# Sums of squares from the transposed input, and a first projection block scaled in two parts

## The reference, cut to what matters

```python
def rms_norm(x, w):
    xf = x.astype(jnp.float32)
    y = xf * lax.rsqrt(jnp.mean(xf * xf, axis=-1, keepdims=True) + EPS)
    return (y * w.astype(jnp.float32)).astype(x.dtype)
...
    h = rms_norm(x, norm_mix_w)
    proj = h @ w_in
```

## Time and profile before

| | |
|---|---|
| median of three runs | 2597.7 us (2597.64 to 2598.22) |
| the profiled execution | 2597.84 us, its span 2596.0 us |
| busy, share of the span | TensorE 98%, VectorE 84%, ScalarE 59%, GpSimd 13% |
| end of the first projection in the chain of waits | 41.82 us |

### The profile page before, as it was taken

One profiled execution on the slowest core, in us unless ns is written; L12 is line 12 of the kernel. 1 busy time (PEld: TensorE's weight loads), 2 busy tenths in 40 slices (PEclk: granted clock), 3 DMA queues, 4 the chain that ended last, 5 costly groups with the idle time before them and its releaser, 6 DMA issues.

```text
span 2596.0 us, 34033 instructions
## 1 busy us (share of the span) xinstructions
PE 2547.8 (98%) x13255; PEld 1981.7 (76%) x13255; DVE 2184.8 (84%) x2451; ACT 1537.9 (59%) x1773; POOL 334.6 (13%) x409
## 2 busy tenths in 40 slices
PE   7999999999999999899999999999999999999998
PEld 7898899889988888676767767766767677666665
DVE  5789888988887344899999999999999999999997
ACT  3444444454435121577777777777777777777775
POOL 0322332233321000000000000000000000000000
PEclk9999999999999999899999999999999999999999
DMA  4233233322447343999999999999999999999995
GB/s 157 70 117 122 89 101 104 130 92 95 135 135 260 131 150 114 373 394 375 379 372 381 377 370 379 376 377 374 374 381 372 376 376 378 375 377 371 373 377 208
DMA packets 72046, 705.22 MB, mean 272 GB/s; under 512 B 9616, under 2 KB 13840, under 8 KB 49360
## 3 DMA queue, kind: packets, MB, share of 16 engines
q1 hardware_dynamic: 48576, 628.95, 62.4%
q0 software_dynamic: 13952, 55.55, 6.9%
q10 hardware_dynamic: 9360, 18.55, 1.9%
HBM read 669.36 MB, written 33.67 MB: 271 GB/s over the span
## 4 chain that ended last, share of the span: by engine, by line
PE 95%; DVE 2%; DMA 1%; ACT 1%; issue 1%; ACTq 0%; POOL 0%; DVEq 0%; POOLq 0%
PE p_gu L2296 38%; PE p_y L2323 19%; PE pp L1042 17%; PE pp L1249 5%; PE pp L1086 5%; PE pp L1268 2%; PE pdg L1137 2%; PE p_h L2308 1%; PE off_banks L1120 1%; PE pp L1351 1%; PE ptr L1104 1%; PE off_banks L1134 1%; PE off_banks L1132 1%; DVE room L1452 0%; PE ptr L1285 0%
## 5 line engine op out<-in xcount | busy, mean ns | idle before, releaser
L2196 DVE TENSOR_TENSOR wl<-raw,wh 128x2048 fp32r<-128x2048 f32 x528 | 1194.1, 2290 | 115.9 <-ACT wh L2115 105.7
L2115 ACT ACTIVATE wh<-raw 128x2048 fp32r<-128x2048 f32 x528 | 991.0, 1911 | 235.0 <-PE p_y L2323 224.2
L2296 PE MATMUL p_gu<-wh,xh 128*96 128x512 f32 x1408 | 565.8, 402 | 0.0
L2296 PE MATMUL p_gu<-wh,xl 128*96 128x512 f32 x1408 | 555.1, 394 | 0.0
L2296 PE MATMUL p_gu<-wl,xh 128*96 128x512 f32 x1408 | 553.0, 393 | 0.0
L1042 PE MATMUL pp<-h_hi,wx_hi 128*128 128x256 f32 (+1 forms) x864 | 307.0, 355 | 3.5 <-DVE zs L1468 3.0
L2296 PEld LDWEIGHTS p_gu<-wl,xh 128*96 128x96 f32 x1408 | 227.2, 161 | 100.0
L2296 PEld LDWEIGHTS p_gu<-wh,xh 128*96 128x96 f32 x1408 | 227.3, 161 | 88.4 <-DVE wl L2196 1.2
L1042 PE MATMUL pp<-h_hi,wx_lo 128*128 128x256 f32 (+1 forms) x864 | 293.8, 340 | 0.0
L1042 PE MATMUL pp<-h_lo,wx_hi 128*128 128x256 f32 (+1 forms) x864 | 292.7, 339 | 0.0
L2296 PEld LDWEIGHTS p_gu<-wh,xl 128*96 128x96 f32 x1408 | 227.2, 161 | 83.2
(11 more groups left out here) (290 smaller groups left out, 3724.5 us busy)
## 6 DMA issues: line engine op xcount, KB each, us to landing
raw<-in_w_e SPq DMA_DIRECT2D x176, 3072.0 KB, 11.1
w_raw<-in_w_x SPq DMA_DIRECT2D x48, 512.0 KB, 3.5
dec<-acs POOLq DMA_DIRECT2D x48, 512.0 KB, 4.8
w_raw<-in_w_g SPq DMA_DIRECT2D x24, 512.0 KB, 3.5
g_tab<-gx POOLq DMA_DIRECT2D x8, 1152.0 KB, 5.9
w_raw<-in_w_s SPq DMA_DIRECT2D x16, 512.0 KB, 3.6
gx<-fo ACTq DMA_DIRECT2D x16, 384.0 KB, 3.0
ys<-yt ACTq DMA_DIRECT2D x14, 384.0 KB, 2.7
```

What stands on the lines that cost most here:

```text
L2115: act.activation(wh[:, n % 2, at:at + hi - lo], raw[:, n % RAW, lo:hi], ACT.Copy).then_inc(s_wh, 1)
L2196: dve.tensor_tensor(wl[:, n % 2, to], raw[:, n % RAW, lo:hi], wh[:, n % 2, to].bitcast(F32), ALU.subtract).then_inc(s_wl, 1)
L2296: mm = pe.matmul(p_gu[n % 2][0:SLOTS, 0:w], xx[:, side, k * SLOTS:(k + 1) * SLOTS], ww[:, n % 2, k * w:(k + 1) * w], start=(k == 0 and i = ...
```

## The change

The rows of x are not loaded any more. The squares are made from the transposed blocks: ScalarE squares each hT[k] into `sqT` (the last block in two parts, 512 and 256 tokens), VectorE adds the eight squares up block by block, TensorE multiplies the result for each 128 tokens by one column of ones, which sums over the partitions, and VectorE scales that sum (`ssq_x`); GpSimd keeps only the power. The transfers go out as six blocks of xT, the first weight block, two more blocks, the second weight block. The first block k = 0 is scaled, split and multiplied in two parts (tokens 0 to 511 and 512 to 767), each with its own count on the semaphores. The warm-up matmuls are placed anew: 13 on ones when the fourth block has landed, 5 behind the sums, 8 behind the broadcast. The wait for the second weight block's low part moves into the first part of the projection, and the Exp of a_log behind the copies.

```diff
@@ sync
-            for c in range(NT):
-                sp.dma_start(x_rows[:, c], A["x"][c]).then_inc(m_x[c], 16)
             for k in range(KD):
-                if 1 <= k <= 2:
-                    sp.dma_start(raw[:, k - 1], A["w_x"][0, k - 1]).then_inc(s_raw[k - 1], 16)
                 sp.dma_start(hT[:, k], A["xT"][k]).then_inc(m_xT[k], 16)
+                if k == 5:
+                    sp.dma_start(raw[:, 0], A["w_x"][0, 0]).then_inc(s_raw[0], 16)
+            sp.dma_start(raw[:, 1], A["w_x"][0, 1]).then_inc(s_raw[1], 16)
@@ gpsimd
-            pool.wait_ge(s_ssq, NT)
+            pool.wait_ge(s_neg, 1)
+            pool.wait_ge(s_rstd, 1)
             pool.sem_inc(s_go, 1)
-            row = Steps(pool, s_rstd)
-            row(pool.tensor_scalar(ssq_x[:], ssq_x[:], 1.0 / D, EPS, ALU.mult, ALU.add))
-            pool.wait_ge(s_neg, 1)
-            row(pool.tensor_tensor(rstd_x[:], ssq_x[:], neg_half[:], ALU.pow))
+            pool.tensor_tensor(rstd_x[:], ssq_x[:], neg_half[:], ALU.pow).then_inc(s_rstd, 1)
@@ scalar
-            for c in range(NT):
-                act.wait_ge(m_x[c], 16)
-                act.activation(x_rows[:, c, :], x_rows[:, c, :], ACT.Square, accum_out=ssq_x[:, c:c + 1]).then_inc(s_ssq, 1)
+            for k, lo, hi in squares:
+                act.wait_ge(m_xT[k], 16)
+                act.activation(sqT[:, k, lo:hi], hT[:, k, lo:hi], ACT.Square).then_inc(s_sqT, 1)
+            high(weight(0, 0))
+            high(weight(0, 1))
+            for i, (k, lo, hi) in enumerate(shares):
+                act.wait_ge(s_hT, i + 1)
+                act.activation(h_hi[:, k, lo:hi], hT[:, k, lo:hi], ACT.Copy).then_inc(s_hh, 1)
             act.wait_ge(m_const, 96)
             act.activation(ea[:], alog[:], ACT.Exp).then_inc(s_act, 1)
@@ tensor
+            pe.wait_ge(s_ones, 1)
+            pe.wait_ge(m_xT[3], 16)
+            for _ in range(13):
+                pe.matmul(pp[0][:, 0:P], ones[:], ones[:], start=True, stop=True)
+            for i, (lo, hi) in enumerate(parts):
+                pe.wait_ge(s_ssum, KD - 1 + i)
+                for c in range(lo // P, hi // P):
+                    mm = pe.matmul(p_ss[:, c:c + 1], sqT[:, KD - 1, c * P:(c + 1) * P], ones[:, 0:1], start=True, stop=True)
+            mm.then_inc(s_ssq, 1)
             pe.wait_ge(m_const, 96)
+            keep_warm(5, pp[0][:, 0:P])
+            pe.wait_ge(s_rstd, 2)
+            for lo, hi in parts:
+                for c in range(lo // P, hi // P):
+                    mm = pe.matmul(p_bc[:, c * P:(c + 1) * P], rstd_x[:, c:c + 1].to_broadcast([P, P]), ident[:],
+                                   start=True, stop=True)
+                mm.then_inc(s_rows, 1)
             keep_warm(8, pp[0][:, 0:P])
...
-            keep_warm(24, pp[0][:, 0:P])
-            pe.wait_ge(s_wl, weight(0, 1) + 1)
-            for k in range(KD):
-                pe.wait_ge(s_hl, k + 1)
+            pe.wait_ge(s_wl, weight(0, 0) + 1)
+            for i, (k, lo, hi) in enumerate(shares):
+                pe.wait_ge(s_hl, i + 1)
                 for j in range(2):
+                    if i == 0 and j == 1:
+                        pe.wait_ge(s_wl, weight(0, 1) + 1)
@@ vector
             dve.wait_ge(m_const, 96)
+            for i, (k, lo, hi) in enumerate(squares[1:]):
+                dve.wait_ge(s_sqT, i + 2)
+                if i:
+                    dve.wait_ge(s_ssum, min(i, KD - 2))
+                dve.tensor_tensor(sqT[:, k, lo:hi], sqT[:, k - 1, lo:hi], sqT[:, k, lo:hi], ALU.add).then_inc(s_ssum, 1)
+            dve.wait_ge(s_ssq, 1)
+            dve.tensor_scalar(ssq_x[:], p_ss, 1.0 / D, EPS, ALU.mult, ALU.add).then_inc(s_rstd, 1)
             low(weight(0, 0))
             low(weight(0, 1))
```

More of the change, by code:

```diff
@@ L163, in mixer @@
                 e = Alloc(nc, first)
-                x_rows = e.sb("x_rows", [P, NT, D])
+                sqT = e.sb("sqT", [P, KD, T])
                 hT = e.sb("hT", [P, KD, T])
@@ L241, in mixer @@
         p_bc = off_banks[:, 0:T]
+        p_ss = pdg_bank[:, 0:NT]
         p_dt, p_f, p_b, p_tot = (t[:, 0:NT * NH].rearrange("p (c n) -> p c n", c=NT)
@@ L282, in mixer @@
         s_pb, s_pt, s_cp, s_ch, s_picks, s_ia, s_idx = a.sems("c_pb", "c_pt", "c_cp", "c_ch", "c_picks", "c_ia", "c_idx")
-        m_x = a.sems(*[f"m_x{c}" for c in range(NT)])
         m_small, m_const, m_acs = a.sems("m_small", "m_const", "m_acs")
         m_xT = a.sems(*[f"m_xT{k}" for k in range(KD)])
-        s_ssq, s_rstd, s_rows, s_hT = a.sems("s_ssq", "s_rstd", "s_rows", "s_hT")
+        s_sqT, s_ssum, s_ssq, s_rstd, s_rows, s_hT = a.sems(
+            "s_sqT", "s_ssum", "s_ssq", "s_rstd", "s_rows", "s_hT")
         s_dt, s_dve, s_act, s_cum, s_cumT, s_copy = a.sems("s_dt", "s_dve", "s_act", "s_cum", "s_cumT", "s_copy")
@@ L289, in mixer @@
         s_neg, s_absv, s_ones, s_dA, s_de = a.sems("s_neg", "s_absv", "s_ones", "s_dA", "s_de")
-        prepared = (*m_x, *m_xT, m_small, s_ssq, s_rstd, s_rows, s_hT, s_dt, s_dve, s_act, s_cum, s_cumT, s_copy,
+        prepared = (*m_xT, m_small, s_sqT, s_ssum, s_ssq, s_rstd, s_rows, s_hT, s_dt, s_dve, s_act, s_cum, s_cumT, s_copy,
                     s_hh, s_hl, s_neg, s_absv, s_ones, s_dA, s_de)
+        parts = ((0, SEQS[0]), (SEQS[0], T))
+        shares = (*((0, *part) for part in parts), *((k, 0, T) for k in range(1, KD)))
+        squares = (*((k, 0, T) for k in range(KD - 1)), *((KD - 1, *part) for part in parts))
         def by_group(t):
@@ L959, in _ @@
             act.dma_start(alog[:], A["a_log"].partition_broadcast(P)).then_inc(m_const, 16)
-            for c in range(NT):
-                act.wait_ge(m_x[c], 16)
-                act.activation(x_rows[:, c, :], x_rows[:, c, :], ACT.Square, accum_out=ssq_x[:, c:c + 1]).then_inc(s_ssq, 1)
+            for k, lo, hi in squares:
[6 more added lines that the diff above has]
+                act.activation(h_hi[:, k, lo:hi], hT[:, k, lo:hi], ACT.Copy).then_inc(s_hh, 1)
             act.wait_ge(m_const, 96)
             act.activation(ea[:], alog[:], ACT.Exp).then_inc(s_act, 1)
-            high(weight(0, 0))
-            high(weight(0, 1))
-            for k in range(KD):
-                act.wait_ge(s_hT, k + 1)
-                act.activation(h_hi[:, k, :], hT[:, k, :], ACT.Copy).then_inc(s_hh, 1)
             act.wait_ge(s_zero, 1)
@@ L1334, in residual @@
                           start=True, stop=True).then_inc(s_ia, 1)
-            pe.wait_ge(m_const, 96)
-            keep_warm(8, pp[0][:, 0:P])
[L1338 to L1343, removed]
-            keep_warm(24, pp[0][:, 0:P])
-            pe.wait_ge(s_wl, weight(0, 1) + 1)
@@ L1348, in _ @@
+            for i, (k, lo, hi) in enumerate(shares):
+                pe.wait_ge(s_hl, i + 1)
                 for j in range(2):
-                    for n0, n1 in ((0, SEQS[0]), (SEQS[0], T)):
-                        for i, (w, h) in enumerate(three(wx_hi, wx_lo, h_hi, h_lo)):
+                    if i == 0 and j == 1:
+                        pe.wait_ge(s_wl, weight(0, 1) + 1)
+                    for n0, n1 in [(n0, n1) for n0, n1 in parts if lo <= n0 and n1 <= hi]:
+                        for x, (w, h) in enumerate(three(wx_hi, wx_lo, h_hi, h_lo)):
@@ L1351, in _ @@
                             mm = pe.matmul(pp[j][:, n0:n1], w[:, j, k * P:(k + 1) * P], h[:, k, n0:n1],
-                                           start=(k == 0 and i == 0), stop=(k == KD - 1 and i == 2))
+                                           start=(k == 0 and x == 0), stop=(k == KD - 1 and x == 2))
                     if k == KD - 1:
@@ L1869, in _ @@
             dve.wait_ge(m_const, 96)
+            for i, (k, lo, hi) in enumerate(squares[1:]):
[5 more added lines that the diff above has]
+            dve.tensor_scalar(ssq_x[:], p_ss, 1.0 / D, EPS, ALU.mult, ALU.add).then_inc(s_rstd, 1)
             low(weight(0, 0))
             low(weight(0, 1))
[L1872 to L1880, removed]
+            dve.wait_ge(m_const, 96)
+            for i in range(len(shares) + 1):
+                if i < len(shares):
+                    k, lo, hi = shares[i]
+                    if k == 0:
+                        dve.wait_ge(s_rows, i + 1)
+                    dve.scalar_tensor_tensor(out=hT[:, k, lo:hi], in0=hT[:, k, lo:hi], scalar=nmix[:, k:k + 1],
+                                             in1=p_bc[:, lo:hi], op0=ALU.mult, op1=ALU.mult).then_inc(s_hT, 1)
+                if i:
+                    k, lo, hi = shares[i - 1]
+                    dve.wait_ge(s_hh, i)
+                    dve.tensor_tensor(h_lo[:, k, lo:hi], hT[:, k, lo:hi], h_hi[:, k, lo:hi].bitcast(F32), ALU.subtract)\
                        .then_inc(s_hl, 1)
```

## The result

The changed kernel takes 2603.4 us (median of 22 runs, 2599.9 to 2604.6) against 2597.8 us for the kernel before (22 runs, 2595.4 to 2600.6). The ratio is 1.0021, with a 95% interval of 1.0016 to 1.0027: 5.5 us slower, 4.2 to 7.0. The forecast was 2.5 us slower: the direction is right and the size is half of the measured one. The measured time lies inside the whole range (2596.3 to 2603.5) by 0.1 us only, and outside the 2599.3 to 2601.2 of the forecast's own case, and the range reached that far for the sake of tables as late as before (13.4 us), which landed at 12.4; that it holds is partly luck. "Within 0.2%" had a chance of 0.87, and the measured ratio stands on that line, a hair over it. Of the rivals, the gain did not come, and the one with the low clock was true up to the broadcast and not in the projection.

A forecast was written before the change was run, and what follows sets the result against it. The end of the first projection's 96 matmuls (41.82 us) was taken to move everything behind it one to one; T 26.3 + 18.0 gave 44.35, +2.5 us, so 2600.2 us, with a range of 2596.3 to 2603.5.

The forecast's parts named there:

- the forecast's own case: Whole kernel: 2.5 us slower, 2600.2 us, own range 2599.3 to 2601.2; chance 0.45.
- tables as late as before: Rival at the start: alog still lands at 13.4 us, the rest as forecast; +4.45, 2602.1 us; chance 0.10.
- the gain: Rival before the adds: tables land by 9 to 10 us and do not gate them; -1.1, 2596.6 us; chance 0.17.
- the one with the low clock: Rival on TensorE: clock stays low into the projection, which ends at 49.4; +7.5, 2605.2 us; chance 0.10.
- The table wait: Head of VectorE's program: adds queue behind all six tables, start 11.5 us; squares alone would allow an earlier end, 2 us lost.
- One table for one piece: Transfer queues: tables and large pieces alternate, so alog lands behind the sixth xT, at 11.45 us instead of 13.4.
- The slow spot: Transfers at 10 to 11 us before the change: 128 GB/s, which could vanish and give 1 us more.
- The sums at the low clock: TensorE's one-column matmuls after some 5 us idle: 0.22 us per record at half clock, result at 20.95 us.
- Power: GpSimd's pow after the scaling: 1.34 us as before, ending at 22.75; VectorE's low parts covered by the broadcast wait.
- When the clock comes back: TensorE: dense work since 18.2 us brings the clock up by 23.3, so the broadcast's first 8 records cost 0.9.
- The split: First block in two parts: brings 0.8 plus 0.45 us, but TensorE then waits 1.0 us once behind k=0.
- T: Time the first h_lo of the projection's first block is ready, forecast 26.3 us; projection end forecast as T + 18.0.

The follow-up runs named there:

- no table wait: The changed kernel with VectorE's adds no longer behind the wait for the six tables; 2600.4 us, ratio 1.0007 to the kernel before.
- low parts early: The changed kernel with both low parts of the weights made on VectorE before it waits for the sum over partitions; 2602.6 us, ratio 1.0019.
- no split: The changed kernel with the first block scaled, copied and subtracted as one piece of 768 columns; 2603.2 us, ratio 1.0020.
- long warm-up: The changed kernel with 36 instead of 13 warm-up matmuls on ones; 2601.0 us, ratio 1.0017.
- all on the change: The changed kernel with broadcast tables late, no table wait before the adds, 20 warm-up matmuls on ones, one low part before the sum wait; 2597.5 us, ratio 1.0000.

## Why the prediction was right or wrong

- **The bound.** Right: the end of the first projection decides, one to one in the medians (table above), and the 24 warm-up matmuls hid 1.9 us where I had 2.0.
- **The table wait.** Right in kind, shown by taking it away (2.9 us at the sums). Mis-sized: alog at 11.45 forecast, 12.42 measured. The sixth xT landed at 11.5, as worked out; alog came 0.9 behind it and not 0.4. One table for one piece was the right choice over a fixed 10 us: alog's 8.9 us from issue to landing were 10.0 before. The Trainium skill ("DMA: Bandwidth & Descriptors", Queues, rings and completion order) has each engine change queues packet by packet; the trace agrees with it. The distance is no constant: in the four other kernels with the same transfers alog came 0.4 to 1.4 us behind the sixth xT. The slow spot, which I only kept as a possible 1 us, was the tables' own.
- **The adds.** 7.0 forecast, 7.08 measured (1.06 from start to start, not 0.99; the parts a little less).
- **The sums at the low clock.** 2.45 forecast behind the last add, 2.73 measured; at the high clock 1.50. That the clock falls was right, and was chosen from the earlier trace rows.
- **Power.** Mis-sized: 1.34 forecast, 2.08 measured. I counted the low parts as covered by the wait for the broadcast, which they were, and gave nothing to their work beside GpSimd; ahead of the sum they leave the power at 1.33 us. The broadcast started at 24.87 instead of 23.2: alog, the sums and the power are 1.0 + 0.3 + 0.7 us later than forecast, of which the wait behind five warm-up matmuls that I had put last hid 0.4.
- **When the clock comes back.** The largest error. I took 5.1 us from the start of the one-column records, as in before from its first warm-up, and so 23.3; it was 26.9. Their later start does not explain it: 19.57 + 5.1 would be 24.7, just ahead of the broadcast, and it took 7.3 us. In the three other traces in which the clock was low, or fell, as these records began it took 6.3 (no table wait), 8.5 (low parts early) and 8.2 us (no split). The broadcast's first eight records took 2.09 instead of 0.9 us. The one-column matmuls with a gap ahead of them did not hold the clock in the long warm-up either; why it took until 26.9 here is not isolated.
- **The split.** Right: gap behind the first k, T + 18.0 forecast, 18.2 measured. The net gain is 0.55 us or less by experiment, where the lead it takes away costs the rest.
- **Sum.** From T = 26.3 to 29.2: broadcast start 1.7 late, broadcast 1.2 longer, 0.1 in the steps; 44.35 became 47.40. The rival "low clock" was right for the warm-up and the broadcast's first eight records and wrong for the projection (49.4), before which the clock was back; its ten per cent should have been more, and with it the chance of over 0.2%. The range held because it went up to 2603.5 for another reason, tables as late as before.

The profiled execution is 6.8 us longer, not 5.6. The difference arises at places that the change does not touch, and in both directions. At the first of the earlier trace rows the changed kernel is only 3.8 us late (1041.70 against 1037.90), and near 1100 us it is 6.8 late (VectorE's hid_lo at 1106.98 against 1100.18). In between TensorE waits for the gather of the first expert's tokens, as in the last of the earlier trace rows. The changed kernel has this, with that wait in it:

```profile
1064.00:1068.00 4.00, 1.91 (x11) 1.91 (x12) 1.64 (x1) 2.24 (x2) 0.23 (x2) 0.56 0.47 118
```

and the kernel before, 4 us earlier in its own time, this:

```profile
1060.00:1064.00 4.00, 2.46 (x24) 2.46 (x25) 1.80 (x2) 3.06 (x3) 0.62 (x3) 1.00 0.49 116
```

In four of the ten traces (the change, low parts early, no split, all on the change) the clock falls in or just behind that wait, and against before they lose 3.0, 1.4, 1.0 and 2.6 us from the first of the earlier trace rows to 1100 us; in the other six it does not fall, and they change by 0.6 at most. The gap was 3.67, 4.09, 2.60 and 2.96 us in those that fell, and 3.17, 3.36, 2.70, 3.46, 3.21 and 3.40 in those that did not, so its length alone does not decide. With the scatter near 100 and 790 us this is why a profiled execution and a median can differ by 2 us.

## What to carry to other kernels

Before removing a transfer from the start of a kernel, ask what stands behind it in the chain: here a small table on another queue was the head, and the 3 MB that went were replaced by 12.4 us of serial steps from alog to the broadcast (adds, sum over partitions, a round trip through three engines), where before there were 3.8. A wait for "all tables" at the head of an engine's program gates everything that is put behind it later; give late-used tables their own semaphore, and load broadcast tables when the large transfers are through. Warm-up matmuls are worth reading as slack: if the chain runs through them, their number is the first thing to change.

## What the runs showed of the hardware

- Two 32 KB tables broadcast to 128 partitions, behind four others on a second queue, cut the transfers of the whole core from about 400 to between 102 and 220 GB/s for about 2 us (7.5 to 9.5); without them the square of the seventh block began at 12.1 instead of 13.8 us.
- A matmul record against one column costs about as much as one against 128 columns: 0.125 us at 2.4 GHz (1.50/12; 128 columns: 5.36/48 = 0.112), 0.227 at 1.2 GHz (2.72/12; 128 columns: 0.237). A stretch of them behind a 2 us gap did not keep the clock up.
- A two-input VectorE subtraction stretches a tiny GpSimd power from 1.33 to 2.06 us, one that overlaps it for 0.9 us as much as two.
- After a gap of 2.6 to 4.1 us the clock may stay or fall (6 against 4 traces at the same place), so a plan that needs it has to leave no such gap.
